# Attention keys: each head projected onto both partition halves, instead of a swap of halves behind the projection

## The reference

```
q, k, v = split of h @ w_in                       # h: 512 x 1024
q = rms_norm(q.reshape(b, s, 16, 64), q_norm_g)   # 16 query heads of 64
k = rms_norm(k.reshape(b, s, 4, 64), k_norm_g)    # 4 key heads of 64
q, k = partial_rope(q, cos, sin), partial_rope(k, cos, sin)
scores = einsum('bnqhgd,bnkhd->bnhgqk', qb, kk)   # 4 query heads share a key head
```

## Time and profile before

| | us |
|---|---|
| median of 3 runs | 2938.89 |
| lowest and highest | 2935.47, 2940.91 |
| the profiled execution, its own time | 2940.91 |
| its span in the profile | 2938.9 |

### The profile page before, as it was taken

One profiled execution on the slowest core, in us unless ns is written; L12 is line 12 of the kernel. 1 busy time (PEld: TensorE's weight loads), 2 busy tenths in 40 slices (PEclk: granted clock), 3 DMA queues, 4 the chain that ended last, 5 costly groups with the idle time before them and its releaser, 6 DMA issues.

```text
span 2938.9 us, 42006 instructions
## 1 busy us (share of the span) xinstructions
PE 2669.1 (91%) x16822; PEld 2174.0 (74%) x16822; DVE 1154.0 (39%) x2079; ACT 1002.2 (34%) x2012; POOL 861.6 (29%) x602
## 2 busy tenths in 40 slices
PE   4999899999988888888788889999998999999999
PEld 3887778777866555545677758999998887777777
DVE  4653565433232112211335664142245776612212
ACT  3334444333232211111423443423323555532231
POOL 0001355322340123200222212646541011365553
PEclk8989999999998999999899978999999999999999
DMA  3321011232333999999121102333331211133331
GB/s 102 87 74 45 21 37 30 72 100 79 98 132 154 422 426 426 426 418 380 46 85 37 44 15 58 87 94 94 87 91 54 59 51 38 49 86 94 100 93 65
DMA packets 313955, 364.13 MB, mean 124 GB/s; under 512 B 10001, under 2 KB 287505, under 8 KB 289185
## 3 DMA queue, kind: packets, MB, share of 16 engines
q1 hardware_dynamic: 313760, 361.42, 35.5%
HBM read 359.29 MB, written 2.10 MB: 123 GB/s over the span
## 4 chain that ended last, share of the span: by engine, by line
PE 72%; DMA 8%; DVE 8%; ACT 5%; POOL 4%; issue 3%; DVEq 0%; ACTq 0%; SPq 0%; POOLq 0%
DMA early<-in_w_up_e 8%; PE bank L1715 5%; PE bank L2176 5%; PE bank L2177 5%; PE bank L2178 5%; PE bank L440 5%; PE bank L442 5%; PE bank L441 5%; PE bank L2607 4%; PE bank L2608 4%; PE bank L2609 4%; POOL split L2153 2%; PE bank L1013 1%; PE bank L2405 1%; PE bank L2869 1%
## 5 line engine op out<-in xcount | busy, mean ns | idle before, releaser
L2153 POOL TENSOR_TENSOR split<-keep,split 128x1024 fp32r<-128x1024 f32 x144 | 353.9, 2461 | 351.5 <-ACT split L2127 351.5
L2176 PE MATMUL bank<-x_hi,split 128*128 128x264 f32 (+1 forms) x1280 | 402.0, 314 | 15.3 <-POOL split L2153 8.1
L2177 PE MATMUL bank<-x_lo,split 128*128 128x264 f32 (+1 forms) x1280 | 394.9, 309 | 0.0
L2178 PE MATMUL bank<-x_hi,split 128*128 128x264 f32 (+1 forms) x1280 | 394.0, 308 | 0.0
L1715 PE MATMUL bank<-early 128*64 128x256 f32 x2048 | 234.8, 383 | 50.7 <-DMA early<-in_w_up_e 22.3
L2127 ACT ACTIVATE split<-keep 128x1024 fp32r<-128x1024 f32 x192 | 200.2, 1050 | 224.9 <-PE bank L2609 210.8
L2176 PEld LDWEIGHTS bank<-x_hi,split 128*128 128x128 f32 x1280 | 244.4, 191 | 38.9 <-issue 18.0
L1715 PEld LDWEIGHTS bank<-early 128*64 128x64 f32 x2048 | 169.9, 137 | 128.8 <-issue 58.5
L2177 PEld LDWEIGHTS bank<-x_lo,split 128*128 128x128 f32 x1280 | 244.6, 191 | 10.7 <-issue 0.2
L2178 PEld LDWEIGHTS bank<-x_hi,split 128*128 128x128 f32 x1280 | 243.6, 190 | 10.9
L2645 DVE TENSOR_TENSOR mlp<-mlp,bank 128x264 f32<-128x264 f32 (+1 forms) x96 | 49.5, 516 | 328.9 <-ACT mlp L2624 328.9
(11 more groups left out here) (462 smaller groups left out, 6108.9 us busy)
## 6 DMA issues: line engine op xcount, KB each, us to landing
early<-in_w_gate_e SPq DMA_DIRECT2D x64, 1024.0 KB, 11.2
early<-in_w_up_e SPq DMA_DIRECT2D x64, 1024.0 KB, 11.5
early<-in_w_down_e SPq DMA_DIRECT2D x64, 1024.0 KB, 11.5
early<-in_w_in SPq DMA_DIRECT2D x68, 512.0 KB, 3.7
keep<-in_mlp_w_in SPq DMA_DIRECT2D x64, 512.0 KB, 3.9
keep<-in_mlp_w_out SPq DMA_DIRECT2D x64, 512.0 KB, 3.9
keep<-in_a_w_qkv SPq DMA_DIRECT2D x24, 512.0 KB, 3.8
early<-in_w_ssd_out SPq DMA_DIRECT2D x16, 512.0 KB, 3.9
```

The costliest lines, as they stand in the source:

```text
L2153: e.tensor_tensor(lo, x, whole(hi), ALU.subtract).then_inc(*u.free(sig_, "lo", n))
L2176: e.matmul(o, hi[:, k, :], XH2[:, k, n0:n1], start=k == 0, stop=False, skip_group_check=True)
L2177: e.matmul(o, hi[:, k, :], XL2[:, k, n0:n1], start=False, stop=False, skip_group_check=True)
L2178: m = e.matmul(o, lo[:, k, :], XH2[:, k, n0:n1], start=False, stop=k == 7, skip_group_check=True)
```

## The change

The keys come as four pieces of 64 columns instead of two of 128. When a piece of 64 columns is split, ACT and DVE read each 64-column row twice, with a step of 0 over the copies, and write it as 128 columns. So the 24 matmuls of a key turn give one head on both halves of the partitions. There are four key turns, and the tile of keys is indexed by the head. The two swap products and their copies are gone. The stage has 16 turns instead of 14, and the wait of the mix stage for the swap is gone.

```diff
-        for i in range(2):
-            piece(("k", i), win, 0, 8, 6176 + 128 * i, 128)
+        for i in range(4):
+            piece(("k", i), win, 0, 8, 6176 + 64 * i, 64)
@@ piece_parts
+            if nc_ == 64:
+                x = x[:, 0:512].rearrange("p (k c) -> p k c", c=64).unsqueeze(2).to_broadcast([128, 8, 2, 64])
+                return [x] + [a.rearrange("p (k a c) -> p k a c", a=2, c=64) for a in (w[:, 0:1024], w[:, 1024:2048])]
@@ qkv
-            return KT[:, 2 * t, :] if t < 2 else QT[:, t - 2, :]
+            return KT[:, t, :] if t < 4 else QT[:, t - 4, :]
-            for t in range(14):
+            for t in range(16):
-                if 0 <= t - 4 < 2:
-                    b, x = XR.take("swap", t - 4), KT[:, 2 * (t - 4), :]
...
-                    for half in range(2):
-                        m = e.matmul(b.ap[64 * half:64 * half + 64, :], C["ident"][:, 64 - 64 * half:128 - 64 * half], x,
-                                     start=True, stop=True, skip_group_check=True)
-                if 0 <= t - 2 < 10:
+                if 0 <= t - 2 < 12:
-                if 0 <= t - 1 < 10:
+                if 0 <= t - 1 < 12:
...
-                if 0 <= t - 4 < 2:
-                    b = XR.of("swap", t - 4)
-                    e.wait_ge(*K.pe.to("swap", t - 4))
-                    e.activation(KT[:, 2 * (t - 4) + 1, :], b.ap[:, :], ACT.Copy).then_inc(*b.free(K.act, "swap", t - 4))
@@ mix
-            e.wait_ge(*K.dve.to("v", 13))
-            e.wait_ge(*K.act.to("swap", 1))
+            e.wait_ge(*K.dve.to("v", 15))
-                            m = e.matmul(bs[bb].ap[:, hh * w:hh * w + w], QT[pr, h // 2, cols(n_, 128)], KT[pr, kv // 2 * 2 + (bb != kv % 2), k0:k0 + w],
+                            m = e.matmul(bs[bb].ap[:, hh * w:hh * w + w], QT[pr, h // 2, cols(n_, 128)], KT[pr, kv, k0:k0 + w],
```

More of the change, by code:

```diff
@@ L754, in qkv_out @@
         def qkv_out(t):
-            return KT[:, 2 * t, :] if t < 2 else QT[:, t - 2, :]
+            return KT[:, t, :] if t < 4 else QT[:, t - 4, :]
         def qkv_ahead(t):
-            n = AT["k", t] if t < 2 else AT["q", t - 2] if t < 10 else AT["v", 1]
+            n = AT["k", t] if t < 4 else AT["q", t - 4] if t < 12 else AT["v", 1]
             return min(n + 2, Z_FIRST - 1)
@@ L769, in qkv_pe @@
                     e.wait_ge(s, n)
-                if t < 2:
+                if t < 4:
                     n = AT["k", t]
                     dense(e, n, b.ap[:, :], xk).then_inc(*WS1.of(n).free(K.pe, "mm", t))
-                elif t < 10:
-                    n = AT["q", t - 2]
+                elif t < 12:
+                    n = AT["q", t - 4]
                     dense(e, n, b.ap[:, :], xk).then_inc(*WS1.of(n).free(K.pe, "mm", t))
                 else:
-                    ns, c = [AT["v", 0], AT["v", 1]], slice(t * 128 - 1280, t * 128 - 1152)
+                    ns, c = [AT["v", 0], AT["v", 1]], slice(t * 128 - 1536, t * 128 - 1408)
                     for n in ns:
@@ L785, in qkv_pe @@
                         m = e.matmul(o, XH[:, k, c], lo[:, k % 4, :], start=False, stop=k == 7, skip_group_check=True)
-                    m.then_inc(*(WS1.of(ns[0]).free(K.pe, "mm", t) if t == 13 else K.pe.up("mm", t)))
-                    if t == 13:
+                    m.then_inc(*(WS1.of(ns[0]).free(K.pe, "mm", t) if t == 15 else K.pe.up("mm", t)))
+                    if t == 15:
                         WS1.of(ns[1]).frees.update(WS1.of(ns[0]).frees)
-                if 0 <= t - 4 < 2:
-                    b, x = XR.take("swap", t - 4), KT[:, 2 * (t - 4), :]
-                    for s, n in b.before:
-                        e.wait_ge(s, n)
-                    e.wait_ge(*K.dve.to("rotated", t - 4))
-                    for half in range(2):
-                        m = e.matmul(b.ap[64 * half:64 * half + 64, :], C["ident"][:, 64 - 64 * half:128 - 64 * half], x,
-                                     start=True, stop=True, skip_group_check=True)
-                    m.then_inc(*K.pe.up("swap", t - 4))
-                if 0 <= t - 2 < 10:
+                if 0 <= t - 2 < 12:
                     b = XR.take("rot", t - 2)
@@ L811, in qkv_act @@
         def qkv_act(e):
-            for t in range(14):
+            for t in range(16):
                 piece_hi(e, qkv_ahead(t))
-                if t < 10:
+                if t < 12:
                     b, x, q = BR.of("qkv", t), HBX.take(t), HBQ.take(t)
@@ L842, in qkv_dve @@
                     q.frees.update(x.frees)
-                if 0 <= t - 1 < 10:
+                if 0 <= t - 1 < 12:
                     x, q = HBX.of(t - 1), HBQ.of(t - 1)
-                    g = C["kg"] if t - 1 < 2 else C["qg"]
+                    g = C["kg"] if t - 1 < 4 else C["qg"]
                     e.wait_ge(*K.act.to("rs", t - 1))
                     e.scalar_tensor_tensor(out=x.ap, in0=x.ap, scalar=g, in1=q.ap, op0=ALU.mult, op1=ALU.mult).then_inc(*K.dve.up("normed", t - 1))
-                if t >= 10:
+                if t >= 12:
                     b = BR.of("qkv", t)
                     e.wait_ge(*K.pe.to("mm", t))
-                    e.tensor_copy(VT[:, t - 10, :], b.ap[:, 0:256]).then_inc(*b.free(K.dve, "v", t))
+                    e.tensor_copy(VT[:, t - 12, :], b.ap[:, 0:256]).then_inc(*b.free(K.dve, "v", t))
         def qkv_pool(e):
             e.wait_ge(*L.act.to("cos"))
-            for t in range(10):
+            for t in range(12):
                 x = HBX.of(t)
@@ L1021, in mix_act @@
             table(e, SET_EXP_TANH)
-            e.wait_ge(*K.pe.to("rot", 9))
+            e.wait_ge(*K.pe.to("rot", 11))
             for i, name in enumerate(("ident", "negbig")):
@@ L1153, in mix_pool @@
             e.wait_ge(*D.act.to("done"))
-            e.wait_ge(*K.dve.to("rotated", 9))
+            e.wait_ge(*K.dve.to("rotated", 11))
             for what, i in MIX:
```

## The result

| | before | changed |
|---|---|---|
| median (lowest to highest), us | 2938.72 (2935.47 to 2940.91), 4 runs | 2955.97 (2953.51 to 2960.24), 4 runs |
| profiled execution, its own time | 2940.91 | 2953.50 |
| its span | 2938.9 | 2951.7 |

The changed kernel takes 1.0053 of the time before, with a 95% interval of 1.0039 to 1.0066. The forecast was +12.0 us, 2950.9, in a range of 2945.5 to 2956.5. The median is +17.2 and lies at the upper edge of the range; the profiled execution is +12.6 over that of before (span +12.8). The +17.2 rests on four executions. The ratio of 1.0053 is about +15.6 us, and six more executions of the changed kernel on record lie between 2949.05 and 2956.29; over all ten the median is 2953.39, which is +14.7.

The account below looks back on a forecast made before the run. PE was taken to bound the qkv stage: two new turns +14.40 us, two removed swaps -2.41, splits and transfers 0, together +11.99 us on the median 2938.89, giving 2950.9 us in a range of 2945.5 to 2956.5.

Parts of the forecast that it names:

- What bounds the stage: qkv stage: PE's queue sets its length; other engines' work is free within waits of some 3.4 and 2.5 us.
- The swap, -2.41: qkv stage: removing two swaps from PE shortens their two turns by 1.20 and 1.21 us, together 2.41 us.
- The two turns, +14.40: qkv stage: two more full key turns on PE at 7.20 us each add 14.40 us.
- Rival 4: qkv stage: new turns cheaper than full ones, sum +8.55 us, 2947.4; chance 4%.
- The splits and the transfers, 0: Key pieces: repeated-row splits on ACT and DVE and half-size transfers stay hidden in waits, cost 0.
- Rival 3: Key splits: repeated-row reads are slow and exposed, up to +9.1 us more, 2960.0; chance 3%.
- The shift reaches the end: Expert stretch: its first transfer waits for the compute before it, so the stream moves by the same 12 us.
- rival 2: Expert stretch: the DMA-bound stream absorbs the delay, no change, 2938.9; chance 3%.
- every stage should keep its length: From the first expert transfer, leaving near 875 us, onward: no stage changes in length.
- Rival 1: Mix stage: clock drops fall elsewhere and win back up to 16.2 us, 2934.7; chance 3% in full form.
- The partial effect: Mix stage: shifted clock drops change the time by some 3 us of either sign, likelier than the full rival 1.
- My sign for it: Mix stage: a mean clock other than 0.94 by more than a hundredth would show the prediction wrong.

Follow-up runs that it names:

- the two 16-turn kernels: The changed kernel with the swap kept in turns 4 and 5 (2952.72 us, ratio 1.0049), and the changed kernel unedited (2951.96 us when timed again).
- the plain keys: The changed kernel with key pieces fetched as 128 columns and split without the repeated row; 2953.97 us, ratio 1.0048.
- kernels with the old order: The 14-turn kernel before, without its swap (2936.74 us, ratio 0.9994) or with the swap made by DMA (2934.77 us, ratio 0.9980).
- the second set: The changed kernel timed again, unedited, against the kernel before; 2951.96 against 2938.47 us, ratio 1.0036.

## Why the prediction was right, point by point

**What bounds the stage.** Confirmed. PE alone set the stage's length; two extra roundings a turn on ACT left it as it was, five did not. How the prediction read the waits (everyone waits for PE, PE for nobody) is what the runs bear out.

**The swap, -2.41.** Confirmed alone (62.9 against 65.3 us) and as the difference of the two 16-turn kernels (79.6 and 77.2). Taking the price from the turn instead of from the swap's own 2 x 1.01 us was right: the 0.20 us in the rotation behind it is real and goes with the 64-column form. The swap's own products would have given +12.38; the stage's +11.9 alone, in round tenths, already speaks for the turn's price, and 62.9 us without swap settles it.

**The two turns, +14.40.** Confirmed: 79.6 - 65.3 = 14.3. Rival 4, cheaper turns (+8.55), falls with it, since every turn is 7.20 us.

**The splits and the transfers, 0.** Confirmed, by the plain keys and by the durations of 1.04 and 1.23 us. Rival 3 falls.

**The shift reaches the end.** Confirmed for a shift of this size. The first expert transfer left 15.1 us later in the first profile and 12.1 us later (875.5) in the second, and the expert stretch behind it was 594.8 and 595.5 us long against 595.5 before; rival 2 falls. With five more roundings the transfer left at 895.9 and the stretch was 590.1 us: in that one execution a longer delay was partly swallowed. That "every stage should keep its length" from there on did not come out: the last stretch took 1.5 us more, and the sum had no term for it.

**The clock.** Rival 1 in its full form, a gain of 12 us and more, did not come. The partial effect "of either sign, some 3 us" is there as scatter: +2.3 us in the mix stage of the first profile, -0.7 in that of the second, -3.1 in the second block's attention in both. The -3.1 is no gain from the change, since kernels with the old order show it too. My sign for it does not work: I had asked for a mean clock off 0.94 by more than a hundredth. The first profile showed 0.94 with 2.3 us more, the second 0.96 with 0.7 us less, and the qkv stage in front was equally long in both.

**The size in the medians.** The profiled executions moved by 12.6, the medians by 17.2. That 12.6 lies so close to 12.0 is partly luck: outside the stage +1.0, +2.3, -0.7, -3.1 and +1.5 us leave only some 0.9. The term that I had too small is the spread of the runs. I took 2.7 us from three runs that lay 5.4 us apart; 15 runs of the same kernel on one chip lie 10.4 us apart, and two sets of runs of the changed kernel gave +17.2 and +13.5. The stage moved by 12 us in both of its profiles. What lies above that is about 1.5 us in the last stretch, which both profiles show, and scatter; that the rest is scatter alone rests on the second set and the two overlapping intervals, and is not shown run by run.

## What to carry to other kernels

Where one engine is busy for a whole stage and nobody makes it wait, as here, an edit costs that stage what it adds to the engine's queue: price it by the length of a turn with and without it, not by the edit's own instructions. Computing a duplicate (two more turns of 7.20 us) replaced a move (two swaps of 1.20 us) on the very engine that had no time to spare; a move is better given to an idle queue, here the DMA. When the effect is near the scatter of whole runs, the distance between two instructions in the stage settles it to a tenth of a microsecond. The distances of the other stages belong beside it, in more than one trace of each kernel: they show what cancels, and what the sum has left out.

## What the runs showed of the hardware

The same kernel's mix stage took 271.8 us in one execution and 268.8 in another, with granted clocks of 0.94 and 0.96; this alone is a quarter of the effect under study. The output's last four transfers of 512 KB took 3.2 us to landing in the kernel before and 4.4 and 4.5 us in the changed one, from a cause that stays open. Two products of 64 columns on the two halves of the output took 1.01 us together where one product of 128 columns took 0.86, and made the 128-column product behind them 0.20 us longer. Reading a source row twice with a step of 0 cost neither ACT nor DVE anything (1.04 and 1.23 us, as without it). Four transfers from one half of the partitions to the other took 2.47 us of SP's queue and nothing of the compute engines. Behind a wait of 2.69 us PE's clock was 0.81 over the next 8.80 us; behind the wait of 1.17 us at 275.59 it was 1.00 over the next turn (276.50 to 285.10).
